# Products of the identity with the constants, ahead of five waits of a layer

## The reference, cut to what matters

```python
for l in range(2):
    h = rmsnorm(x, g_pre[l]) * (1 + scale) + shift
    u_val, u_gate, g_conv, c_q, c_kv, k_idx, w_idx, g_attn = split(h @ w_in[l])
    # convolution branch
    a = u_val * sigmoid(u_gate)
    y_conv = silu(layernorm(causal_depthwise_conv(a, 31 taps))) @ w_pw2 * silu(g_conv)
    # attention branch
    cq = rmsnorm(c_q)
    q, q_idx = cq @ w_uq, cq @ w_qidx           # 8 heads x 128, 8 index heads x 64
    score = sum_h w_idx[h] * relu(q_idx[h] @ k_idx.T)
    sel = top 256 keys of each query by score
    y_attn = softmax(q @ kv.T / sqrt(128) + bias, over sel) @ kv @ w_uv * silu(g_attn)
    x = x + gate * rmsnorm(concat(y_conv, y_attn) @ w_out[l])
```

## Time and profile before

| | |
|---|---|
| median of 3 runs | 3044.73 us (3043.07 to 3046.05) |
| the profiled execution | 3046.43 us |
| its span | 3044.6 us |
| PE busy | 2860.1 us, 94% of the span |
| DVE busy | 1953.3 us, 64% |
| ACT busy | 1323.3 us, 43% |
| POOL busy | 1280.0 us, 42% |
| mean granted clock of TensorE | 0.98 |

### The profile page before, as it was taken

The page is one execution under the profiler, slowest core; times in us unless marked ns, Lnnn a source line. Parts: engine busy times, 40 slices in busy tenths (PEclk is TensorE's granted clock), DMA queues, the critical chain, the costliest instruction groups (busy, mean ns, idle before and its releaser), DMA issues.

```text
span 3044.6 us, 49166 instructions
## 1 busy us (share of the span) xinstructions
PE 2860.1 (94%) x19746; PEld 1749.1 (57%) x19746; DVE 1953.3 (64%) x3140; ACT 1323.3 (43%) x2341; POOL 1280.0 (42%) x1060
## 2 busy tenths in 40 slices
PE   7889998999979988999999999999999999999998
PEld 3438776874429667864466565664764444444443
DVE  3785997763589996644875665666663654444445
ACT  3353654652366646643344554454543322122222
POOL 1302482010602580012545846767661635555551
PEclk9999999999989999999999999999999999999999
DMA  8223241002201340021101111201122201111111
GB/s 292 110 70 122 84 154 52 12 22 104 94 14 43 125 139 29 12 87 59 67 29 42 70 42 42 70 31 66 43 85 110 70 28 56 56 56 44 54 44 74
DMA packets 50898, 213.45 MB, mean 70 GB/s; under 512 B 4680, under 2 KB 9968, under 8 KB 34032
## 3 DMA queue, kind: packets, MB, share of 16 engines
q1 hardware_dynamic: 42288, 195.63, 18.5%
q10 hardware_dynamic: 8384, 14.68, 1.4%
HBM read 190.36 MB, written 19.94 MB: 69 GB/s over the span
## 4 chain that ended last, share of the span: by engine, by line
PE 41%; DVE 3%; POOL 3%; ACT 2%; issue 1%; DMA 0%; ACTq 0%; POOLq 0%; DVEq 0%
PE big L284 7%; PE big L286 7%; PE big L285 7%; PE banks L284 4%; PE banks L286 4%; PE banks L285 4%; PE banks L1183 3%; POOL w_lo L596 2%; PE banks L1162 0%; PE banks L1153 0%; PE banks L1134 0%; PE banks L1164 0%; PE banks L1170 0%; DVE arena L2567 0%; DVE arena L2568 0%
## 5 line engine op out<-in xcount | busy, mean ns | idle before, releaser
L653 POOL TENSOR_TENSOR w_lo<-stage,w_hi 128x512 bf16<-128x512 f32 x340 | 429.7, 1295 | 367.3 <-ACT w_hi L1390 367.0
L646 POOL CAST w_hi<-stage 128x512 bf16<-128x512 f32 x252 | 179.6, 753 | 781.4 <-PE big L286 588.5
L284 PE MATMUL big<-w_hi,ht_hi 128*128 128x256 bf16 (+2 forms) x1280 | 358.0, 288 | 22.7 <-DVE arena L1913 4.7
L596 POOL TENSOR_TENSOR w_lo<-stage,w_hi 128x512 bf16<-128x512 f32 x174 | 249.6, 1445 | 263.6 <-ACT w_hi L1590 263.6
L285 PE MATMUL big<-w_lo,ht_hi 128*128 128x256 bf16 (+2 forms) x1280 | 357.9, 288 | 0.0
L286 PE MATMUL big<-w_hi,ht_lo 128*128 128x256 bf16 (+2 forms) x1280 | 357.8, 287 | 0.0
L284 PE MATMUL big<-ht_hi,w_hi 128*128 128x512 bf16 x816 | 310.2, 380 | 24.7 <-POOL w_lo L596 8.7
L286 PE MATMUL big<-ht_hi,w_lo 128*128 128x512 bf16 x816 | 310.0, 380 | 0.0
L285 PE MATMUL big<-ht_lo,w_hi 128*128 128x512 bf16 x816 | 309.8, 380 | 0.0
L284 PE MATMUL big<-arena,w_hi 128*128 128x512 bf16 (+1 forms) x716 | 222.5, 328 | 21.4 <-DVE arena L2154 8.4
L285 PE MATMUL big<-arena,w_hi 128*128 128x512 bf16 (+1 forms) x716 | 222.6, 328 | 0.0
(11 more groups left out here) (395 smaller groups left out, 7144.2 us busy)
## 6 DMA issues: line engine op xcount, KB each, us to landing
stage<-in_w SPq DMA_DIRECT2D x130, 1024.0 KB, 4.8
arena<-in_w_ada SPq DMA_DIRECT2D x48, 512.0 KB, 4.4
arena<-in_x SPq DMA_DIRECT2D x16, 512.0 KB, 9.2
xs<-arena SPq DMA_DIRECT2D x16, 512.0 KB, 2.6
arena<-xs SPq DMA_DIRECT2D x16, 512.0 KB, 7.2
gt<-arena ACTq DMA_DIRECT2D x16, 256.0 KB, 2.5
arena<-gt ACTq DMA_DIRECT2D x16, 256.0 KB, 2.6
out_x<-arena SPq DMA_DIRECT2D x8, 512.0 KB, 2.6
```

The lines of the kernel that those rows point to most:

```text
L284: pe.matmul(out, ah, bh, start=start, stop=False, skip_group_check=onto)
L596: return pool.tensor_tensor(lo, x, hi, ALU.subtract)
L646: pool.tensor_copy(w_flat[0][:, w0 + c0:w0 + c1], stage[:, n % RAW_RING, c0:c1]).then_inc(s_w_hi_split, mark(s_w_hi_split, n, q))
L653: ins = pool.tensor_tensor(w_flat[1][:, w0 + c0:w0 + c1], stage[:, n % RAW_RING, c0:c1], w_flat[0][:, w0 + c0:w0 + c1], ALU.subtract)
```

## The change

A helper `bridge(g, n)` issues n products of the identity with the first 512 columns of the constants, in f32, into the first 512 columns of a tile that PE has just taken. Nobody reads them: the next product into that tile begins with start=True and overwrites them. It is called at five places of a layer: 5 products ahead of the wait before the index queries (the take moves ahead of that wait), 6 and 2 ahead of the first and the second pair of the pointwise product, 4 ahead of the wait of the first logits, and 4 ahead of the wait of the last `turn_y`. In `logits` and `turn_y` the take moves ahead of the wait for all blocks and heads.

```diff
--- before.py
+++ after.py
@@ -670,6 +670,11 @@
                         between()
                 ins.then_inc(s_gemm, mark(s_gemm, *key))

+            def bridge(g, n):
+
+                for i in range(n):
+                    pe.matmul(g[:, 0:512], ident, con[:, 0:512], start=True, stop=True)
+
             def chunk_used(l, name, sem):

                 seen[("used", CHUNK_AT[(l, name)])] = (sem.name, counts[sem.name])
@@ -902,9 +907,11 @@
                                   [x[:, 0, 1024 + k * 8:1024 + k * 8 + 8] for x in w], k == 0, k == KT - 1)
                 ins.then_inc(s_turn, mark(s_turn, "wi", l))

-                pe.wait_ge(s_latent_dve, when(s_latent_dve, "cq_lo", l, 1))
                 for n in range(4):
                     g = take(pe, "big", "qi", l, n)
+                    if n == 0:
+                        bridge(g, 5)
+                        pe.wait_ge(s_latent_dve, when(s_latent_dve, "cq_lo", l, 1))
                     for half in range(2):
                         for k in range(2):
                             ins = mm3(pe, g[:, half * 512:(half + 1) * 512],
@@ -960,6 +967,7 @@
                 w = chunk(l, "pw2", 4)
                 for n0 in (0, 2):
                     pair = [take(pe, "big", "pw2", l, n) for n in (n0, n0 + 1)]
+                    bridge(pair[0], 6 if n0 == 0 else 2)
                     for k in range(4):
                         pe.wait_ge(s_conv_dve, when(s_conv_dve, "ln_lo", l, k))
                         for n, g in zip((n0, n0 + 1), pair):
@@ -986,8 +994,10 @@

                 def logits(tb, h):
                     N = (tb + 1) * P
+                    g = take(pe, "big", "lg", l, tb, h)
+                    if tb == 0 and h == 0:
+                        bridge(g, 4)
                     pe.wait_ge(s_qt_lo, when(s_qt_lo, l, tb))
-                    g = take(pe, "big", "lg", l, tb, h)
                     near = max(0, N - 2 * P)
                     q = [x[:, h, :] for x in QT[tb % 2]]
                     cuts = sorted({0, near, N} | {512} if N > 512 else {0, near, N})
@@ -1025,8 +1035,10 @@

                 def turn_y(tb):

+                    g = take(pe, "big", "yt", l, tb)
+                    if tb == NT - 1:
+                        bridge(g, 4)
                     pe.wait_ge(s_ya, when(s_ya, l, tb))
-                    g = take(pe, "big", "yt", l, tb)
                     for c in range(4):
                         ins = pe.transpose(g[:, c * P:(c + 1) * P], YR[tb % 2][:, c * P:(c + 1) * P], ident)
                     ins.then_inc(s_gemm, mark(s_gemm, "yt", l, tb))
```

## The result

| | before | after |
|---|---|---|
| median, measured together | 3046.16 us (3041.33 to 3050.64, 16 runs) | 3050.4 us (3046.61 to 3055.74, 16 runs) |
| the profiled execution | 3046.43 us | 3053.36 us |
| its span | 3044.6 us | 3051.5 us |
| mean granted clock | 0.980 | 0.984 |

The ratio is 1.0016, 95% interval 1.0009 to 1.0022: slower by 2.7 to 6.7 us, 4.2 us by the medians. The forecast was 4.8. The clock's mean went up and the kernel got slower all the same.

A forecast was written before the change was run, and what follows sets the result against it. TensorE, busy 94% of the span, was taken as the bound. Layer 0's +1.8 and layer 1's +3.0 us made +4.8 (11.5 over, 6.7 given back), so 3049.5 us against a median of 3044.73; range 3041 to 3055.

The forecast's parts named there:

- The price, 0.86 us a product: At all five places: one added 128x512 f32 product costs 0.86 us at the upper clock level.
- Rival 3: At all groups: a product costs one record, 0.43 us; sum about -8 us, 3036.5 us; chance 8%.
- The first pair: Six products before the pointwise product's first pair outlast the wait: +1.2 us in layer 0, +1.8 in layer 1.
- The middle: Two products in the middle of the pointwise product fill no wait: 1.7 us in the open each layer.
- Index queries: Five products before the index queries start them 5.6 us late, but a faster clock makes up for it: net 0.
- Logits: Four products before the first logits: 0.8 us over, 1.4 or 0.8 given back, net -0.6 and 0.
- rival 2: In the attention, the second low clock stretch is spared too: 2.4 us more given back each layer, 3044.7 us; 15%.
- Transposes: Four products before the last transpose of y: 0.9 us over, 1.4 given back, net -0.5 us each layer.
- Rival 1: Clock falls elsewhere, in the attention's first blocks or later; half of 6.7 us comes back, 3052.9 us; 22%.
- Rival 4: At all groups: they do not hold the clock, all 11.5 us over is paid, about 3062 us; chance 5%.
- The estimate of 0.52 us a product: From the skill page's 131 ns: a product of 0.52 us would let nearly every group end inside its wait.

The follow-up runs named there:

- e3: The changed kernel with 12 products instead of 2 in the middle of the pointwise product; 3069.02 us, ratio 1.0072 to the kernel before.
- e7: The kernel before plus only the six products ahead of the first pair of the pointwise product; 3044.2 us, ratio 0.9993.
- e2: The changed kernel without the 2 products in the middle of the pointwise product; 3047.14 us, ratio 1.0003 to the kernel before.
- e4: The kernel before plus only the five products at the index queries and the moved takes; 3047.02 us, ratio 0.9998.
- e9: e6 plus the change's five products at the index queries; 3034.56 us, ratio 0.9971 to the kernel before.
- e5: e1 with 9 products of 8 columns in place of each group's 3 of 512; 3044.84 us, ratio 0.9998 to the kernel before.
- e8: The changed kernel plus e6's three single products in the attention's first blocks; 3046.91 us, ratio 1.0007 to the kernel before.
- e6: e1 plus three single products a layer in the attention's first blocks; 3037.61 us, ratio 0.9975 to the kernel before.
- e1: The changed kernel with groups cut to 0 (index queries), 3 and 0 (pointwise), 3 (logits), 3 (transpose); 3042.46 us, ratio 0.9989 to the kernel before.

## Why the prediction was right, and where it was off

The forecast of 3049.5 us met 3050.4, and in the main for its reasons: the price, the overruns and the spared stretches are seen each at its place. That it is so close is partly luck. The first logits of layer 0 gave back 1.0 us more than forecast, and a fall of the clock that the sum didn't have took 2.0; the profiled execution, with +6.3 in the layers, is 2.1 us above the 3051.2 that the sum gave for it.

- **The price, 0.86 us a product.** Right: 0.865 in e3's group of 12, 0.88 by whole times. Rival 3 (0.43 us) is out, and with it the only case that made the change clearly faster.
- **The first pair, +1.2 and +1.8.** Right: from the last gate product to the pair's last product it is 1.3 and 1.9 longer, and e7, which has this group alone, shows the same up to the first query product. That the group starts at ScalarE's last read and not where PE falls idle was the step that mattered.
- **The middle, 1.7 in each layer.** Right: 1.8 us each, which with the 1.3 and 1.9 makes the +3.2 and +3.7 of the ledger. Taking them out (e2) brings the kernel from 4.2 to 1.0 us over before, 3.2 for the two layers where 3.4 was expected; in the layers of the profiled executions it is 3.7.
- **Index queries, 0.** Right as a net (-0.2 and +0.2 in the kernel after; e4, e9). Its parts were nearly right: the five products took 6.8 and 7.2 us, forecast 6.8, and the clock came back about 2 us before they ended, forecast 1.9.
- **Logits, +0.8 over and 1.4 or 0.8 given back.** Overrun 0.9. Given back were 2.4 in layer 0 and 0.8 in layer 1. The term for layer 0 was too small. With the same group and the whole second stretch at the lower level, e2 and e3 give back 1.7 and 1.8, so 0.3 or 0.4 of the 1.0 us was a term sized too low; the rest goes with the half of the second low stretch that the kernel after is spared, a part of rival 2 in one layer.
- **Transposes, -0.5 each.** Right within 0.3 us at the place (-0.7 and -0.4). But the sum ended there, and the clock falls at the next wait instead, as shown above.
- **Rival 1, the clock falls elsewhere.** It did in the profiled execution, not in the attention, where the rival looked first, but later, at 780 and again at 1446. The first costs 2 of the 6.3 us in the layers, and without it they would be at 4.3; the second lies in the stretch behind the layers, which is 0.9 longer. In 12 of 14 places the profiles with a group at the last transpose show such a fall, so it is no accident of one execution. How often it happens in the runs that were not profiled stays open; the median is 0.9 us above the forecast.
- **Rival 4, groups that don't hold the clock.** It is out: the clock is at 1.00 behind every group but the queries', which starts at the lower level. The rule of the Trainium skill that transposes with the identity don't count as work for the clock (TensorE: Matmul & The Clock Gate, Part 4: PE-mode transpose) doesn't reach plain products of the identity, by these rows. With 8 columns in place of 512 the clock fell (e5).
- **The estimate of 0.52 us a product.** The prediction says that at this price nearly every group would end inside its wait. Its own rows say otherwise: six products from 454.2 would end at 457.3, past the data at 456.6, and only the logits' and the transposes' groups would end in time. No number of the forecast rests on it.

In sum the change pays some 11 us of overruns (e8 against e6: 10.8 by whole times, 11.0 at the places) for what fewer products in the same places give at no cost (e1), and leaves out the place where three products are worth as much again (e6).

## What to carry to other kernels

A product that only keeps the clock up has the price of a real one as soon as it reaches past its wait. Size a group by distances from start to start, count from the moment when its tile is free and not from when the engine falls idle, and leave out every place where the take itself ends the wait. Then look at where the time given back goes: part of it meets the next wait, the next low stretch can be the larger one, and the clock can fall at a later wait that no group covers. For changes of a few microseconds compare the edited stretch in the traces, and let the whole time only confirm it.

## What was not expected of the hardware

- Summed over windows of 1 us from 80 to 3040, before has 102.4 us at the lower level in 20 stretches, after 78.5 in 16, e6 74.0 in 15, e8 58.0 in 11; each stretch is 3.4, 6.8 or 13.7 us long, but for one of 5.7 in e6 that the end of the span cuts off. The longest, 13.7 us from 1528 in before, lies behind the layers and was not tried.
- Less time at the lower level is not less time. After has 24 us less of it than before and is slower; e8 has the least of all and is no faster than before.
- Records of PE alone did not keep the clock: in e5 PE has 18 records of 8-column products in 2.15 us, the data comes 0.25 us later, and the clock fell as it fell before behind an idle PE.
- The clock can fall behind a wait where another execution of nearly the same program keeps it: at layer 1's first products it fell in after, e1, e2, e3, e6 and e9, and not in before, e4, e5, e7 and e8.
